# Expert weights loaded one by one at the ring's first turn, the scatter as two fp32r products, and a last quarter in halves

## The chip, the cores and the metric

One core of one Trainium2 chip runs the program. The metric is the device time of one execution in microseconds (us), as the median of several runs. The profile is of one execution. TensorE (PE in the rows; PEld is its weight load), VectorE (DVE), ScalarE (ACT), GpSimd (POOL) and SyncE (SP) each work through an own list of instructions and meet through semaphores.

## The reference

One decoder layer on x of 256 tokens by 1024, all float32: a mixer stage (sparse attention, pooling, short convolution, merged by gates and projected), then a mixture of experts, then a final RMSNorm. The change touches the mixture of experts and the first steps of the final norm:

```python
# 4 groups of 8 experts; each token takes one group and the best 2 experts in it
combine = jnp.einsum('nk,nke->ne', top_w, jax.nn.one_hot(expert_id, N_EXPERTS))
for e in range(N_EXPERTS):                       # 32
    h = jax.nn.silu(xt @ w1[e]) * (xt @ w3[e])   # 1024 -> 256
    out = out + combine[:, e:e + 1] * (h @ w2[e])  # 256 -> 1024
```

## The kernel before, in words

**Stages.** The mixer stage fills about the first 207 us. Routing follows to 220.5 us, then the experts. The experts' weights (three matrices of 1 MB for each of 32 experts) are read once, 96 chunks of 1 MB (128 partitions by 2048 float32).

**The ring.** `ring` has 22 slots of one chunk (`SLOTS`, line 42). The first 22 chunks are loaded one by one during the mixer stage as its slots come free (`early`, L508 to L511). All later ones go out in pairs, two chunks in one transfer, in SyncE's loops (L577 to L579, and L588 to L590 for the second half of the experts): the pair (c, c+1) waits until TensorE has counted up `expert_used` for the chunk that sat in the slot of c+1 before (`earlier(c + 1) + 1`). Only the last two chunks of a round go singly (L580 to L582, L592 to L595).

**Blocks.** The experts are worked in 8 blocks of 4 experts (`EB`), each expert with room for 32 tokens (`CAP`), so that a block has 128 rows. Four blocks are a round (`ROUND`), `j` is the block within it, and a round has 48 chunks, 12 for each block: q = 0 to 7 are the rows of w1 and w3 for one eighth of the model's width each, q = 8 to 11 the columns of w2 in four quarters of 256. In each block TensorE (L1736 to L1803) does, in this order:

- transposes of the combine weights of the block's rows (L1742, into bank 1, copied to `cmbT` by VectorE in L1312);
- q = 0 to 7: eight matmuls of 32 columns each group against the chunk (L1758). Before q = 1 and q = 2 it gathers the tokens of the second half of the width (`gather`, L1719, products with the 0/1 matrix `sel`), which VectorE copies (L1309). In the last block of a round two idle matmuls (`keep_busy`, L1368) stand after each of q = 4, 5 and 6;
- gathers 0 and 1 for the next block, after `sel_step`; the transposes of the hidden rows (L1774), for which ScalarE has done the silu (L894) and VectorE the product (L1317); gather 2; ScalarE copies the transposed rows (L896);
- second(0), gather 3, second(1), combine(0), second(2), combine(1), second(3), combine(2), combine(3). `second` (L1785) multiplies a quarter of w2 into bank 4 or 5, ScalarE copies it to `yN` (L901). `combine` (L1795) multiplies the combine weights `cmbT` with `yN` in plain float32 for each token tile t, into bank 6 + t; VectorE adds the result to `h` (L1323). A combine waits for the adds of the combine before it, since there are two banks.

**The end.** When the last quarters are added, ScalarE squares `h` in pieces (L920), GpSimd and VectorE multiply with the final gain (L675, L1349), VectorE sums the mean squares (L1351, L1354), GpSimd takes the power of -0.5 (L677), ScalarE and VectorE scale (L938, L1358), and four transfers write the output (L599, L940).

A matmul in plain float32 shows as two instructions in the trace, one in fp32r as one.

Of the kernel before, what the change touches and what calls it, by code (L numbers as in the profile page):

```python
# [5 lines left out]
ALU = mybir.AluOpType  # L6
# [28 lines left out]
NQT = D // QC  # L35
CAP = 32
# [5 lines left out]
SLOTS = 22  # L42
GATES = HEADS * 3
# [80 lines left out]
def build(nc, x, params, consts, front, projs, small, wgrp, vecs, routerw, routerb, experts, out):  # L124
    with ExitStack() as ctx:
# [103 lines left out]
        yN = gab[:].rearrange("p a c -> p (a c)")  # L229
# [13 lines left out]
        cmbT = vflat[:, 0:256]  # L243
# [31 lines left out]
        expert_in = [sem(f"expert_in{i}") for i in range(SLOTS // 2)]  # L275
        last_in = sem("last_in")
        expert_used = sem("expert_used")
# [98 lines left out]
        yn_done = sem("yn_done")  # L376
        gained = sem("gained")
# [86 lines left out]
        def second_out(qt, rows):  # L464

            return bank[4 + qt % 2][rows, 0:QC]

        def combined(t):

            return bank[6 + t][:, 0:QC]  # L470
# [4 lines left out]
        def _(sp):  # L475
# [104 lines left out]
            for c, sem_in in ((NC - 2, expert_in[AT[NC - 2] // 2]), (NC - 1, last_in)):  # L580
                sp.wait_ge(expert_used, earlier(c) + 1)
                sp.dma_start(ring[:, AT[c]], single(c)).then_inc(sem_in, 16)  # L582
# [4 lines left out]
            with sp.Fori(1, passes * (NB // ROUND)) as r:  # L587
# [4 lines left out]
                for c, sem_in in ((NC - 2, expert_in[AT[NC - 2] // 2]), (NC - 1, last_in)):  # L592
                    sp.wait_ge(expert_used, r * NC + (earlier(c) + 1))
                    sp.dma_start(ring[:, AT[c]], rounds[bass.ds(r % (NB // ROUND), 1), c // NQ, c % NQ // 2, :, c % 2 * ECHUNK:(c % 2 + 1) * ECHUNK]
                                 .rearrange("o p c -> (o p) c")).then_inc(sem_in, 16)  # L595
# [7 lines left out]
        def _(pool):  # L603
# [69 lines left out]
            for qt, c in ((1, slice(0, 2 * QC)), (2, slice(2 * QC, 3 * QC))):  # L673
                pool.wait_ge(add_done, passes * (NT * NQT * NB) + (NT * qt + 1 - NT))
                nc.gpsimd.tensor_tensor(fin[:, 1, c], h[:, 1, c], fing[:, c], ALU.mult).then_inc(gained_most, 1)  # L675
            pool.wait_ge(means_done, 2)
# [3 lines left out]
        def _(act):  # L680
# [226 lines left out]
            with act.Fori(0, passes * NB - 1) as b:  # L907
                hidden(b + 1)
                for qt in range(NQT):
                    second_copy(b + 1, qt)  # L910
# [4 lines left out]
            def last_square(n, t):  # L915

                qt, c0, c1, scratch = ((1, 0, 2 * QC, (kv[:, 512:1024], qflat[:, 0:512])), (2, 2 * QC, 3 * QC, (sl1, hN)),
                                       (3, 3 * QC, D, (flat(selw), flat(hT))))[n]
                act.wait_ge(add_done, passes * (NT * NQT * NB) + (NT * qt + t - NT))
                nc.scalar.activation(scratch[t], h[:, t, c0:c1], ACT.Square,  # L920
# [9 lines left out]
            for n in (1, 2):  # L930
# [4 lines left out]
            act.wait_ge(gained_most, 2)  # L935
# [7 lines left out]
        def _(dve):  # L943
            for s1 in (hn_done,):
                dve.sem_inc(s1, 1)
            dve.sem_inc(add_done, 5)
# [359 lines left out]
            def gathered(b):  # L1306
# [5 lines left out]
                nc.vector.tensor_copy(cmbT, bank[1][:, 0:T]).then_inc(cmb_done, 1)  # L1312

            def through(b):
# [4 lines left out]
                for qt in range(NQT):  # L1319
                    for t in range(NT):  # L1320
                        dve.wait_ge(comb_done, b * (NT * NQT) + (NT * qt + t + 1))
                        hv = h[:, t, qt * QC:(qt + 1) * QC]
                        nc.vector.tensor_tensor(hv, hv, combined(t), ALU.add).then_inc(add_done, 1)  # L1323
# [601 lines left out]
```

## Time and profile before

| | us |
|---|---|
| median of 3 runs | 423.47 |
| the runs | 423.47, 424.98, 423.26 |
| the profiled execution | 424.43 |
| its span | 422.6 |
| TensorE busy (share of the span) | 392.2 (93%) |
| VectorE busy | 200.6 (47%) |
| ScalarE busy | 141.8 (34%) |
| transfers, mean over the span | 332 GB/s |
| first expert matmul | 220.91 |
| last add to h ends | 415.68 |

The profiled execution took 424.43 us, 1.83 us more than its span, the time from the first to the last recorded instruction. All stretches below are counted from the start of the span. The page cuts the span into 40 slices of 10.6 us; the GB/s line gives what the transfers moved in each.

### The profile page before, as it was taken

To read this page: it belongs to the slowest core of one execution; us is meant where nothing else is said; L and a number is where in the kernel's file an instruction comes from. 1 tells how busy PE (TensorE), PEld (TensorE's weight loads), DVE (VectorE), ACT (ScalarE), POOL (GpSimd) and SP (SyncE) were. 2 spreads that over 40 slices of the span, in tenths; PEclk is the share of its full clock that TensorE was granted. 3 is DMA by queue.
4 is the path that set the end of the run, shared out by engine and by line. 5 is a ranking of instruction groups with operands and counts; after the bars stand their busy time and mean duration, and the time that the engine had idled before them with its cause. 6 is when DMAs were issued, how large, how long until landed. Compare 5 with 4: busy or idle time off the path is not lost.

```text
span 422.6 us, 7127 instructions
## 1 busy us (share of the span) xinstructions
PE 392.2 (93%) x2826; PEld 263.9 (62%) x2826; DVE 200.6 (47%) x392; ACT 141.8 (34%) x257; POOL 20.1 (5%) x39
## 2 busy tenths in 40 slices
PE   6999999999999999999989999999999779679792
PEld 5998988677777777878765545453546335135251
DVE  3847574999888595673362323231222203112113
ACT  6734352638555535341430303030303012011014
POOL 3010000200000000000510000000000000000002
PEclk9999999999999999999999999999999989899898
DMA  8999999534352485569987999999999999999962
GB/s 295 421 406 352 399 382 395 198 136 158 106 186 99 152 347 200 205 243 365 420 359 268 433 425 426 410 424 426 426 428 428 426 426 430 426 428 426 430 267 99
DMA packets 16440, 140.29 MB, mean 332 GB/s; under 512 B 2081, under 2 KB 2465, under 8 KB 5025
## 3 DMA queue, kind: packets, MB, share of 16 engines
q1 hardware_dynamic: 15264, 138.07, 81.1%
q10 hardware_dynamic: 1152, 1.88, 1.2%
q8 instruction: 17, 0.28, 0.3%
q14 instruction: 7, 0.05, 0.0%
HBM read 138.90 MB, written 1.05 MB: 331 GB/s over the span
## 4 chain that ended last, share of the span: by engine, by line
PE 73%; DMA 18%; DVE 6%; issue 1%; POOL 0%; ACT 0%; POOLq 0%; DVEq 0%; SPq 0%
DMA ring<-in_experts 17%; PE bank L1758 10%; PE bank L1719 5%; PE bank L1785 5%; PE bank L1795 5%; PE bank L1525 5%; PE bank L1526 4%; PE bank L1527 4%; PE bank L1383 4%; PE bank L1384 4%; PE bank L1385 4%; PE bank L1646 2%; PE bank L1368 2%; PE bank L1647 2%; PE bank L1648 2%; PE bank L1487 1%
## 5 line engine op out<-in xcount | busy, mean ns | idle before, releaser
L1758 PE MATMUL bank<-ring,kv 128*32 128x512 f32 x512 | 65.9, 630 | 12.9 <-DMA ring<-in_experts 12.8
L458 DVE TENSOR_TENSOR part<-ring,part 128x2048 fp32r<-128x2048 f32 (+1 forms) x26 | 57.4, 2213 | 18.7 <-ACT part L451 18.6
L451 ACT CAST part<-ring 128x2048 fp32r<-128x2048 f32 (+1 forms) x26 | 48.0, 1847 | 32.5 <-DMA ring<-in_front 32.5
L1323 DVE TENSOR_TENSOR h<-h,bank 128x256 f32<-128x256 f32 x64 | 26.9, 421 | 60.6 <-PE bank L1795 60.3
L1719 PEld LDWEIGHTS bank<-qcur,att 128*128 128x128 f32 x256 | 31.6, 191 | 24.2 <-issue 24.2
L1758 PEld LDWEIGHTS bank<-ring,kv 128*32 128x32 f32 x512 | 13.7, 112 | 42.1 <-issue 29.7
L1525 PE MATMUL bank<-part,xhi 128*128 128x512 f32 x96 | 39.2, 408 | 0.0
L894 ACT ACTIVATE cw<-bank 128x256 f32<-128x256 f32 x8 | 3.1, 384 | 105.4 <-PE bank L1758 105.4
L1719 PE MATMUL bank<-qcur,att 128*128 128x128 f32 x256 | 38.4, 288 | 0.0
L1527 PE MATMUL bank<-part,xlo 128*128 128x512 f32 x96 | 37.5, 391 | 0.0
L1526 PE MATMUL bank<-part,xhi 128*128 128x512 f32 x96 | 37.5, 391 | 0.0
L1383 PE MATMUL bank<-xhi,part 128*128 128x256 f32 x128 | 36.6, 286 | 0.5 <-DVE xlo L971 0.5
L1785 PE MATMUL bank<-ring,hidT 128*32 128x256 f32 x512 | 34.3, 385 | 2.9 <-DMA ring<-in_experts 2.8
L1795 PE MATMUL bank<-gab,vbd 128*128 128x256 f32 x128 | 36.2, 405 | 0.7
L1384 PE MATMUL bank<-xlo,part 128*128 128x256 f32 x128 | 36.2, 283 | 0.0
L1385 PE MATMUL bank<-xhi,part 128*128 128x256 f32 x128 | 36.2, 283 | 0.0
L1795 PEld LDWEIGHTS bank<-gab,vbd 128*128 128x128 f32 x128 | 21.0, 188 | 16.1 <-DVE h L1323 9.6
L1317 DVE TENSOR_TENSOR vbd<-cw,bank 128x256 f32<-128x256 f32 x8 | 3.4, 420 | 56.2 <-ACT cw L894 56.2
L901 ACT COPY gab<-bank 128x256 f32<-128x256 f32 x32 | 11.9, 372 | 47.9 <-PE bank L1785 47.9
L1383 PEld LDWEIGHTS bank<-xhi,part 128*128 128x128 f32 x128 | 24.5, 192 | 1.7 <-DVE xlo L971 0.9
L1385 PEld LDWEIGHTS bank<-xhi,part 128*128 128x128 f32 x128 | 24.5, 192 | 0.0
L1384 PEld LDWEIGHTS bank<-xlo,part 128*128 128x128 f32 x128 | 24.5, 192 | 0.0
(250 smaller groups left out, 549.9 us busy)
## 6 DMA issues: line engine op xcount, KB each, us to landing
ring<-in_experts SPq DMA_DIRECT2D x35, 2048.0 KB, 27.6
ring<-in_front SPq DMA_DIRECT2D x28, 1024.0 KB, 5.6
ring<-in_experts SPq DMA_DIRECT2D x26, 1024.0 KB, 8.7
ring<-in_front SPq DMA_DIRECT2D x4, 512.0 KB, 6.9
ring<-in_projs SPq DMA_DIRECT2D x4, 512.0 KB, 5.0
ring<-in_front SPq DMA_DIRECT2D x2, 560.0 KB, 8.7
h<-in_x SPq DMA_DIRECT2D x2, 512.0 KB, 3.8
con<-in_vecs ACTq DMA_DIRECT2D x2, 512.0 KB, 7.5
```

The source lines that it names most:

```text
L451: nc.scalar.copy(high(n, half)[:, 0:c].bitcast(F32R), raw(n, half)[:, 0:c]).then_inc(hi_done, 1)
L458: nc.vector.tensor_tensor(low(n, half)[:, 0:c].bitcast(F32R), raw(n, half)[:, 0:c], high(n, half)[:, 0:c], ALU.subtract).then_inc(split_do ...
L1383: mm(dst, whi, ahi, start=start, stop=False)
L1384: mm(dst, whi, alo, start=False, stop=False)
L1385: return mm(dst, wlo, ahi, start=False, stop=stop)
L1525: mm(bank[t][:], XH[:, kk, cols], whi[:, k], start=(kk == 0), stop=False)
L1526: mm(bank[t][:], XH[:, kk, cols], wlo[:, k], start=False, stop=False)
L1527: ins = mm(bank[t][:], XL[:, kk, cols], whi[:, k], start=False, stop=(kk == KT - 1))
L1719: ins = mm(bank[2 + k // 4][:, (k % 4) * P:(k % 4 + 1) * P], xn2[:, t, k * P:(k + 1) * P], flat(sel[:, t]), start=(t == 0), stop=(t == NT ...
L1758: ins = mm(bank[0][CAP * e:CAP * (e + 1)], xgT[:, q, CAP * e:CAP * (e + 1)], expert(j, q, e), start=(q == 0), stop=(q == NQ1 - 1))
L1785: ins = mm(second_out(qt, slice(CAP * e, CAP * (e + 1))), hT[:, ht, CAP * e:CAP * (e + 1)], second_weights(j, qt, ht, e), start=(ht == 0), ...
L1795: mm(combined(t), cmbT[:, t * P:(t + 1) * P], yN[:, qt * QC:(qt + 1) * QC], start=True, stop=True).then_inc(comb_done, 1)
```

## The change

- **Single loads.** The first six transfers at the ring's second turn (chunks 22 to 27 of the first round) go out singly, each after its own slot's `expert_used`. The pairs start at chunk 28.
- **Last quarter in halves.** The w2 columns are worked in five pieces: three quarters of 256 and two halves of 128. The last chunk of a round comes in two transfers of 0.5 MB, each with its own semaphore, in a layout in which each half is contiguous.
- **Moved transposes.** The combine weights' transposes go from the block's start to behind q = 2.
- **Moved gathers.** In the last block of a round the four gathers for the next block stand behind q = 4, 5, 6 and 7, and `keep_busy` is gone there. In the other blocks they stay.
- **Scatter in fp32r.** VectorE makes `cmbT` a 0/1 matrix (rounded exactly in fp32r) and puts each row's combine weight into a column `share` (two instructions where there was one). ScalarE's copy scales by `share` and rounds to fp32r; VectorE computes what the rounding left (`low_part`, new); `combine` adds two fp32r products, of the rounded and of the rest.
- **Order at the end.** VectorE does low_part(p) before the adds of p - 1. In the last block of a round TensorE does second 0, 1, combine 0, 1, second 2, combine 2, second 3, second 4, combine 3, combine 4. The final squares, gains and mean sums have one more piece each.

```diff
+PIECES = ((0, 256), (256, 512), (512, 768), (768, 896), (896, 1024))
+NP = len(PIECES)
+SINGLES = 6
...
-        cmbT = vflat[:, 0:256]
+        cmbT = over("cmbT", [P, T], "vbd")[:]
+        share = stat[:, 40:41]
...
@@ SyncE
-            for c in range(SLOTS, NC - 2, 2):
+            for c in range(SLOTS, SLOTS + SINGLES):
+                sp.wait_ge(expert_used, earlier(c) + 1)
+                sp.dma_start(ring[:, AT[c]], single(c)).then_inc(expert_in[AT[c] // 2] if c % 2 else single_in, 16)
+            for c in range(SLOTS + SINGLES, NC - 2, 2):
                 sp.wait_ge(expert_used, earlier(c + 1) + 1)
                 sp.dma_start(slots_of(c), experts[c // NQ, c % NQ // 2]).then_inc(expert_in[AT[c] // 2], 16)
...
+            def last_chunk(r):
+
+                for i, sem_in in ((0, last_half_in), (1, last_in)):
+                    sp.dma_start(ring[:, AT[NC - 1], i * (SLOT // 2):(i + 1) * (SLOT // 2)],
+                                 halves[bass.ds(r, 1), i].rearrange("o p c -> (o p) c")).then_inc(sem_in, 16)
@@ ScalarE
-            def second_copy(after, qt):
-
-                act.wait_ge(ye_full, after * NQT + (qt + 1))
-                nc.scalar.copy(yN[:, qt * QC:(qt + 1) * QC], second_out(qt, slice(0, P))).then_inc(yn_done, 1)
+            def second_copy(after, p):
+
+                act.wait_ge(ye_full, after * NP + (p + 1))
+                act.wait_ge(cmb_done, after)
+                nc.scalar.activation(yN[:, columns(p)].bitcast(F32R), second_out(p, slice(0, P)), ACT.Copy, scale=share).then_inc(yn_done, 1)
@@ VectorE
-                nc.vector.tensor_copy(cmbT, bank[1][:, 0:T]).then_inc(cmb_done, 1)
+                nc.vector.tensor_scalar(cmbT.bitcast(F32R), bank[1][:, 0:T], 0.0, None, ALU.is_gt)
+                nc.vector.tensor_reduce(share, bank[1][:, 0:T], AX.X, ALU.add).then_inc(cmb_done, 1)
...
+                def low_part(p):
+
+                    dve.wait_ge(yn_done, b * NP + (p + 1) + 1)
+                    nc.vector.scalar_tensor_tensor(low_out(p).bitcast(F32R), second_out(p, slice(0, P)), share, yN[:, columns(p)],
+                                                   ALU.mult, ALU.subtract).then_inc(ylo_done, 1)
...
+                low_part(0)
+                for p in range(1, NP):
+                    low_part(p)
+                    add(p - 1)
+                add(NP - 1)
@@ TensorE
-                    pe.wait_ge(sel_done, b + 1)
-                    pe.wait_ge(hT_done, b + 1)
-                    for t in range(NT):
-                        ins = nc.tensor.transpose(bank[1][:, t * P:(t + 1) * P], flat(selw[:, t]), ident)
-                    ins.then_inc(cmb_full, 1)
...
-                        if j == ROUND - 1 and 4 <= q < NQ1 - 1:
-                            pe.wait_ge(add_done, b * (NT * NQT) + 5)
-                            keep_busy(2, ident, con[:, K_TRI:K_TRI + 2 * P])
-
-                    pe.wait_ge(sel_step, b + 2)
-                    gather(0, 1)
+                        if q == 2:
+                            pe.wait_ge(sel_done, b + 1)
+                            pe.wait_ge(hT_done, b + 1)
+                            for t in range(NT):
+                                ins = nc.tensor.transpose(bank[1][:, t * P:(t + 1) * P], flat(selw[:, t]), ident)
+                            ins.then_inc(cmb_full, 1)
+                        if j == ROUND - 1 and q >= 4:
+                            pe.wait_ge(sel_step, b + 2)
+                            gather(q - 4)
+
+                    if j < ROUND - 1:
+                        pe.wait_ge(sel_step, b + 2)
+                        gather(0, 1)
...
-                        pe.wait_ge(yn_done, b * NQT + (qt + 1) + 1)
-                        pe.sem_inc(expert_used, 1)
+                        pe.wait_ge(ylo_done, b * NP + (p + 1))
+                        if p != NP - 2:
+                            pe.sem_inc(expert_used, 1)
                         for t in range(NT):
-                            pe.wait_ge(add_done, b * (NT * NQT) + (NT * qt + t + 4))
-                            mm(combined(t), cmbT[:, t * P:(t + 1) * P], yN[:, qt * QC:(qt + 1) * QC],
-                               start=True, stop=True).then_inc(comb_done, 1)
+                            pe.wait_ge(add_done, b * (NT * NP) + (NT * p + t + 6))
+                            picked = cmbT[:, t * P:(t + 1) * P].bitcast(F32R)
+                            mm(combined(p, t), picked, yN[:, columns(p)].bitcast(F32R), start=True, stop=False)
+                            mm(combined(p, t), picked, low_out(p).bitcast(F32R), start=False, stop=True).then_inc(comb_done, 1)
 
                     second(0)
-                    gather(3)
-                    for qt in range(1, NQT):
-                        second(qt)
-                        combine(qt - 1)
-                    combine(NQT - 1)
+                    if j < ROUND - 1:
+                        gather(3)
+                    second(1)
+                    combine(0)
+                    if j == ROUND - 1:
+                        combine(1)
+                    second(2)
+                    combine(2 if j == ROUND - 1 else 1)
+                    second(3)
+                    if j < ROUND - 1:
+                        combine(2)
+                    second(4)
+                    combine(3)
+                    combine(4)
```

## Rows read from the trace of the kernel before

**Rows 1.** The page: GB/s in 40 slices; one kind of transfer, size, us to landing

```profile
GB/s 295 421 406 352 399 382 395 198 136 158 106 186 99 152 347 200 205 243 365 420 359 268 433 425 426 410 424 426 426 428 428 426 426 430 426 428 426 430 267 99
...
ring<-in_front SPq DMA_DIRECT2D x28, 1024.0 KB, 5.6
```
**Rows 2.** The chain that ended last, in order of time: start, us, what

```profile
363.18 32.15 DMA ring<-in_experts
...
396.57 2.01 PE bank L1368 x4
```
**Rows 3.** Stretches: length, busy PE, PEld, DVE, ACT, POOL, clock, DMA share, GB/s

```profile
221.00:222.00 1.00, 1.00 (x9) 0.16 (x9) 0.00 (x0) 0.00 (x0) 0.00 (x0) 1.00 0.00 0
397.00:398.00 1.00, 1.00 (x4) 0.68 (x3) 0.00 (x0) 0.00 (x0) 0.00 (x0) 0.50 1.04 442
409.00:410.00 1.00, 1.00 (x8) 0.59 (x11) 0.49 (x2) 0.27 (x1) 0.00 (x0) 1.00 0.08 33
```
**Rows 4.** Timeline, 217 to 225 and 242 us: start, us, engine, line, operation, count, idle before

```profile
217.48 2.02 PE L1728 MATMUL bank<-qcur,att 128*128 128x128 f32 x16 [0.16 <-DVE qcur L1290]
...
219.56 1.28 ACT L894 ACT_TABLE_LOAD   x1 [0.55 <-issue]
...
220.54 0.44 PE L1742 MATMUL bank<-con,otmp 128*128 128x128 f32 x2 [1.04 <-DVE otmp L1298]
...
220.91 1.07 PE L1758 MATMUL bank<-ring,kv 128*32 128x512 f32 x8
...
221.91 1.16 PE L1719 MATMUL bank<-qcur,att 128*128 128x128 f32 x8
...
223.00 1.06 PE L1758 MATMUL bank<-ring,kv 128*32 128x512 f32 x8
...
224.12 0.33 SPq L579 DMA_DIRECT2D ring<-in_experts  x1
...
241.61 1.06 PE L1758 MATMUL bank<-ring,kv 128*32 128x512 f32 x8
```
**Rows 5.** Timeline, 362 to 371 and 404 to 423 us, same columns

```profile
366.04 3.30 PE L1758 MATMUL bank<-ring,kv 128*32 128x512 f32 x16 [3.06 <-DMA ring<-in_experts]
...
404.26 0.38 ACT L894 ACTIVATE cw<-bank 128x256 f32<-128x256 f32 x1 [19.53 <-PE bank L1758]
...
406.12 1.07 PE L1785 MATMUL bank<-ring,hidT 128*32 128x256 f32 x16
...
407.25 0.37 ACT L901 COPY gab<-bank 128x256 f32<-128x256 f32 x1 [1.19 <-PE bank L1785]
...
408.76 1.13 PE L1795 MATMUL bank<-gab,vbd 128*128 128x256 f32 x4
...
409.50 0.85 DVE L1323 TENSOR_TENSOR h<-h,bank 128x256 f32<-128x256 f32 x2 [4.40 <-PE bank L1795]
...
414.10 0.73 PEld L1795 LDWEIGHTS bank<-gab,vbd 128*128 128x128 f32 x4 [0.48 <-DVE h L1323]
...
414.83 0.85 DVE L1323 TENSOR_TENSOR h<-h,bank 128x256 f32<-128x256 f32 x2 [0.36 <-PE bank L1795]
...
416.32 0.16 DVE L1354 TENSOR_TENSOR stat<-stat 128x2 f32<-128x2 f32 x1
416.56 0.71 POOL L677 TENSOR_TENSOR stat<-stat 128x2 f32<-128x2 f32 x1 [1.28 <-DVE stat L1354]
```
**Rows 6.** Groups by line and shape: busy us, mean ns, idle before

```profile
L971 DVE SCALAR_TENSOR_TENSOR xlo<-bank,prm,xhi 128x256 fp32r<-128x256 f32 x8 | 3.5, 477 | 0.1
...
L706 ACT ACTIVATE xhi<-bank,prm 128x256 fp32r<-128x256 f32 x8 | 3.3, 492 | 0.1
...
L1193 DVE TENSOR_TENSOR pcw<-otmp,con 128x128 f32<-128x128 f32 x2 | 0.5, 288 | 0.0
```
**Rows 7.** Timeline of TensorE at 52 us: two fp32r matmuls in a row

```profile
51.89 0.28 PE L1384 MATMUL bank<-xlo,part 128*128 128x256 f32 x1
52.01 0.28 PE L1385 MATMUL bank<-xhi,part 128*128 128x256 f32 x1
```

More of the change, by code:

```diff
@@ L462, in xT, with columns, low_out, second_out @@
             return bank[(0, 1, 2, 3, 6, 7, 5, 5)[k]][:, (k == 7) * T:((k == 7) + 1) * T]
[L464 to L470, printed above, removed]
+        def columns(p):
+            return slice(*PIECES[p])
+        def low_out(p):
+            c0, c1 = PIECES[p]
+            return ylo[c0 // 512][:, c0 % 512:c0 % 512 + c1 - c0]
+        def second_out(p, rows):
+            return bank[4 + p % 2][rows, 0:PIECES[p][1] - PIECES[p][0]]
+        def combined(p, t):
+            return bank[6 + t][:, 0:PIECES[p][1] - PIECES[p][0]]
         block = ctx.enter_context(nc.Block())
@@ L591, in _ @@
                                  .rearrange("o p c -> (o p) c")).then_inc(expert_in[AT[c] // 2], 16)
[L592 to L595, printed above, removed]
+                sp.wait_ge(expert_used, r * NC + (earlier(NC - 2) + 1))
+                next_to_last(r % (NB // ROUND))
+                sp.wait_ge(expert_used, r * NC + (earlier(NC - 1) + 1))
+                last_chunk(r % (NB // ROUND))
             for half, t in ((0, 0), (0, 1), (1, 0)):
@@ L672, in _ @@
             pool.wait_ge(vec_in, 32)
-            for qt, c in ((1, slice(0, 2 * QC)), (2, slice(2 * QC, 3 * QC))):
-                pool.wait_ge(add_done, passes * (NT * NQT * NB) + (NT * qt + 1 - NT))
+            for p, c in ((1, slice(0, 512)), (2, columns(2)), (3, columns(3))):
+                pool.wait_ge(add_done, passes * (NT * NP * NB) + (NT * p + 1 - NT))
                 nc.gpsimd.tensor_tensor(fin[:, 1, c], h[:, 1, c], fing[:, c], ALU.mult).then_inc(gained_most, 1)
-            pool.wait_ge(means_done, 2)
+            pool.wait_ge(means_done, 3)
             nc.gpsimd.tensor_tensor(stat[:, 30:32], stat[:, 28:30], stat[:, 32:34], ALU.pow).then_inc(rstd_last, 1)
@@ L908, in _ @@
                 hidden(b + 1)
-                for qt in range(NQT):
-                    second_copy(b + 1, qt)
+                for p in range(NP):
+                    second_copy(b + 1, p)
                 gathered_copy(b + 1)
@@ L929, in _ @@
             second_copy(blocks, 3)
-            for n in (1, 2):
+            second_copy(blocks, 4)
+            for n in (1, 2, 3):
                 for t in range(NT):
@@ L1775, in _, with second @@
                     ins.then_inc(hT_full, 1)
-                    gather(2)
+                    if j < ROUND - 1:
+                        gather(2)
                     pe.wait_ge(hT_done, b + 2)
-                    def second(qt):
-                        have_expert(j, NQ1 + qt)
+                    def second(p):
+                        if j == ROUND - 1 and p == NP - 2:
+                            pe.wait_ge(last_half_in, bb * 16 + 16)
+                        else:
+                            have_expert(j, NQ1 + PIECES[p][0] // QC)
@@ L1899 @@
         w2.transpose(0, 4, 3, 2, 1, 5).reshape(NB, NQ2, P, ECHUNK)], axis=1)
+    halves = experts[:, NQ - 1].reshape(NB, P, HT * EB, 2, QC // 2).transpose(0, 1, 3, 2, 4).copy()
+    experts[:, NQ - 1] = halves.reshape(NB, P, ECHUNK)
+    ends = np.stack([experts[:, NQ - 2], halves.transpose(0, 2, 1, 3, 4).reshape(NB, P, ECHUNK)], axis=1).reshape(NB, P, 2 * ECHUNK)
     experts = experts.reshape(NB, NQ // 2, 2, P, ECHUNK).transpose(0, 1, 3, 2, 4).reshape(NB, NQ // 2, P, 2 * ECHUNK)
+    experts[ROUND - 1::ROUND, NQ // 2 - 1] = ends[ROUND - 1::ROUND]
     arrays = {
```

67 lines of the change are left out of this document (42 added, 25 removed).

## The prediction

> **What bounds the kernel now.** I read the slices first: from the 23rd on, the transfers move 424 to 434 GB/s (two slices 410 and 426) until the last two [rows 1]. In the slices before, at 211 to 232 us, there is a hole of 359 and 268. So the experts are bound by reading 96 MB, and what counts is where this stream starts, and what follows its last bytes. The stretches show both ends: nothing moves at 221 to 222 us, and the stream is almost over at 409 to 410 [rows 3]. The timeline says why: the first transfer of the ring's second turn is issued at 224.12, right after chunk 1 is used up at 224.06; chunk 0 had been used at 221.98 [rows 4]. The chain of waits shows the other end: TensorE stands before transfers from 363.18 to 395.33, and from there to the last add it is TensorE's own work that sets the time [rows 2, 5]. A pair of chunks lands every 4.89 us (waits that end at 366.04 and at 395.38 are six pairs apart [rows 2, 5]), so 2.45 us a chunk. By that step the last pair of w1 and w3 lands at 400.27, the first pair of w2 at 405.16, chunk 10 at 407.61 and chunk 11 at 410.05. Yet second(0) starts only at 406.12 and the last add ends at 414.83 + 0.85 = 415.68 [rows 5]: TensorE is late there, by gathers, idle matmuls and plain float32 products.
>
> **Start of the stream.** Two things come earlier. The single load needs chunk 0 alone: 224.06 - 221.98 = 2.08 us. And the transposes that stood ahead of chunk 0 waited for VectorE's weights until 220.54 [rows 4]; now TensorE can begin chunk 0 once it has left the first gathers (217.48 + 2.02 = 219.50) and entered its loop. No row shows that entry alone on TensorE. Bounds: 0, so 219.5, and the old wait's end, 220.5. ScalarE needs 0.55 us between its copy and the loop's first instruction [rows 4]; I take 0.5, so chunk 0 starts at 220.0 in place of 220.91. Sum 2.08 + 0.9 = 3.0 us, with 2.5 and 3.5 as ends. The following singles keep the stream fed: chunk 1 is free 2.1 us after chunk 0 (1.0 matmuls and 1.09 gathers [rows 4]), against 2.45 us that a chunk takes, chunk 2 two more after that, later ones about 1 us apart. TensorE's 20.7 us for an early block (220.91 to 241.61 [rows 4]) against 12 x 2.45 = 29.4 of the stream leaves the later pairs free early too. The six singles themselves cost nothing as long as others are queued: that is the slice of 420 GB/s, where singles run as well [rows 1].
>
> **Extra work in the other blocks: 0.** VectorE gets a reduction and five low parts more a block (some 2.6 us), and four fp32r products in place of four plain halves of products save TensorE about half of 1.06 us per combine [rows 5, 7]. It all lies beside the stream, as every block has 29.4 us. By the ladder worked out below, a block's last combine is issued some 5.5 us after its last pair lands, and 4.2 us more go to the next block's q = 0 and 1 with their gathers: 9.7, just within the 9.8 us to the landing of q = 2. Were it a few us more, the 2.9 us that TensorE waits for q = 4 would still hide it. The transposes behind q = 2 make VectorE wait there for them, and behind that wait stand the 0/1 matrix, the sum (0.42 each, as every 256-wide op), and the selection for the next block, for which the last block's gathers now wait: it is ready about 2.5 us after q = 2 lands, and the first gather comes over 5 us after it. On SyncE's queue five transfers more are issued (0.33 us each [rows 4]), all well ahead of their data's turn.
>
> **The last block.** All landings come 3.0 us earlier: q = 4 at 392.4, q = 6 at 397.3, second(0)'s chunk at 402.2, the last half at 407.1. Idle matmuls go (they took 2.01 us at half clock once [rows 2]), and gathers of 0.55 us take their place between chunks. From 397.3: 1.0 + 0.5 + 1.0 us for q = 6, a gather and q = 7, 0.13 to the silu, and as now 1.86 from there to second(0) (404.26 to 406.12 [rows 5]): ready at 401.8. So second(0) starts at 402.2, by its transfer, 3.9 us earlier than now.
>
> Then a longer ladder. second takes 1.0 us, the copy starts 0.13 behind it [rows 5]. The copy is now scaled from a column: 0.37 as a plain copy [rows 5], 0.49 in the row of the same form [rows 6]; I take 0.48. low_part is the form of L971, 0.48 [rows 6]; pieces of 128 take 0.38 and 0.33 (VectorE has 0.29 for an op of 128 [rows 6]). Adds 0.42 and 0.29. An fp32r product follows the last by 0.12 and ends 0.28 after its start [rows 7], so an add can start 0.47 behind its combine, where it now is 0.74 [rows 5]. VectorE's end reaches TensorE in 0.06 (an add ends at 414.05, the weight load is at 414.10). No row has an fp32r product of 128 columns; between 0.06 and 0.27 apart, I take 0.10, as its weights' load overlaps as in rows 7. Working it through:
> - second 0 and 1 to 404.20; copy 1 to 404.82; low 1 to 405.35; adds of 0 to 406.11; combine 1 must wait for their banks, to 406.41.
> - second 2 to 407.41. Its chunk landed at 404.6, so the transfer is not the wait. Copy 408.03, low 2 408.56, adds of 1 to 409.32, combine 2 to 409.62.
> - second 3 to 410.21, second 4 to 410.80; both halves are there since 407.1. Copy 3 410.73, low 3 411.11, adds of 2 411.87, low 4 412.20, adds of 3 412.70, combine 4's first product done 412.90, its adds 413.48.
>
> Last add 413.5 in place of 415.7. From the start of second(0) it is 11.3 us now against 9.6 before: the new order gives back 1.7 of 3.9. Behind the last add one more mean step (0.26, the distance of such steps, L1354 at 416.32) less 0.1 for smaller squares: the power starts at 414.5 where it was 416.56 [rows 5], the rest is equal. Span 422.6 - 2.0 = 420.6, time 424.43 - 2.0 = 422.4.
>
> **Against the median.** The profiled run was 0.96 above the median of 423.47. In it the clock was at 0.50 at 397 to 398 [rows 3], which made q = 6 start at 401.1 in place of its landing at 400.3: 0.8 us that the new order does not pay, since it has slack there. I put that to the profiled run alone and the other 0.16 to both: 422.2 us, which is 0.3% under the median. Changes within 0.5% (2.1 us) are about what the measurement can't tell from none.
>
> **A rule to weigh.** Singles ran at the stream's rate where several were queued [rows 1]. The Trainium skill (DMA: Bandwidth & Descriptors, Rules for kernel authors and Anatomy of one DMA) asks for transfers of at least 1 MiB and gives each about 2 us of fixed cost. By that page five more transfers (three for the singles, one half in each round), if none overlapped, would be 10 us more; it adds that issuing early hides the cost, and it speaks against the halves above all.
>
> **Rivals.**
> 1. The ladder is shorter, up to the halves' purpose, that the last bytes set the end. For it: VectorE and ScalarE may overlap more, and low ends of 0.42 and 0.37 for low part and copy take 0.6 off, an entry at 219.5 up to 0.4 more: 421.2. If only the last half at 407.1 counted: 0.6 + 0.5 + 0.4 + 0.4 + 0.6 to the last add at 409.6, and 418.3. Against: second(2) is 1.8 us behind its landing by the ladder. Chance 0.28, 418.3 to 421.3.
> 2. The change gives only the single load's 2.08, since TensorE's loop entry takes the whole microsecond that the moved transposes should free: 0.9 more, 423.1. Chance 0.10.
> 3. Half clock once in the tail. After 3.06 us of idleness 16 matmuls took 3.30 us [rows 5], where 2.0 do at full clock [rows 4]. The gaps between combines (up to 1.6 us) are shorter, but TensorE is only half busy. One such dip costs about 1.6 (3.3 us at half rate): 423.8. Chance 0.08.
> 4. The other side: the clock stays at its lower level (1.2 GHz) from second(0) to the end, as no idle matmuls hold it. TensorE's part of the ladder is 3.6 us of seconds and about 1.8 of combines; doubled, 5.4 more: 427.6. It decides from 3.4 us of TensorE's ladder at that level, over half of it. Chance 0.04.
> 5. Each of the five extra transfers pays alone, at most 5.6 - 2.45 = 3.15 us by a chunk loaded with little else in the queue [rows 1]: 422.2 + 15.8 = 438.0. Chance 0.02.
> The forecast has 0.48.
>
> **Numbers.** Faster by over 0.5% (under 421.35): rival 1 and the lower edge of the forecast, 0.33. Slower (over 425.6): rivals 4 and 5 and a little of 3, 0.08. Within: 0.59. The range 420.0 to 424.3 leaves out the best third of rival 1 and the worst of 3 to 5.
>
> **What would show it.** First load of the second turn at about 221.1 instead of 224.1; the stream's end 3 us earlier; second(0) of the last block near 402.2; second(2) over 1.5 us behind its chunk; the last add near 413.5. It is wrong if TensorE waits for the last half (then the ladder was overpriced), if the copy or low part is far from 0.48, or if the clock in the last 12 us is not 1.0.

## The result, and the profile after

| | before | after |
|---|---|---|
| median (18 runs each) | 424.35 | 425.25 |
| lowest and highest | 423.26, 426.21 | 424.85, 425.96 |
| the profiled execution | 424.43 | 425.27 |
| its span | 422.6 | 422.8 |

The ratio is 1.0023, with a 95% interval of 1.0015 to 1.0032: a loss of 0.9 us that is clear of the spread and smaller than the 0.5% within which the prediction counts a change as none. It is 3 us above the forecast and outside the range. (With 18 runs the kernel before has a median 0.9 above that of the three runs shown first.) Times below are us.

The timeline of after at the start of the experts, and at chunk 27's use in block 2 (start, length, engine, line, operation, count, idle before):

```profile
219.59 1.06 PE L1810 MATMUL bank<-ring,kv 128*32 128x512 f32 x8
...
220.71 2.42 SPq L598 DMA_DIRECT2D ring<-in_experts  x2
...
266.51 0.44 PE L1820 MATMUL bank<-con,otmp 128*128 128x128 f32 x2
...
266.88 4.50 PE L1810 MATMUL bank<-ring,kv 128*32 128x512 f32 x40
...
268.01 2.57 SPq L601 DMA_DIRECT2D ring<-in_experts  x3
```

The first load of the second turn goes out at 220.71, 3.4 earlier than in [rows 4]. But the pair (40, 41) goes out at 268.01, just after TensorE has worked chunk 27 (q = 3 of block 2, from 266.88). The stretches show what lies between (columns as in [rows 3]: length, five engines, clock, DMA share, GB/s); first four long ones, then single microseconds:

```profile
219.00:226.00 7.00, 6.96 (x55) 3.26 (x58) 2.31 (x6) 1.35 (x2) 0.00 (x0) 1.00 0.84 304
226.00:263.00 37.00, 35.55 (x367) 19.31 (x360) 13.88 (x39) 9.33 (x18) 0.00 (x0) 1.00 1.00 417
263.00:272.00 9.00, 9.00 (x77) 3.68 (x76) 2.34 (x6) 0.38 (x1) 0.00 (x0) 1.00 0.88 335
272.00:390.00 118.00, 99.69 (x951) 52.35 (x953) 36.33 (x101) 21.67 (x43) 0.00 (x0) 0.97 1.01 427
...
267.00:268.00 1.00, 1.00 (x12) 0.30 (x13) 1.00 (x3) 0.00 (x0) 0.00 (x0) 1.00 0.61 246
268.00:269.00 1.00, 1.00 (x12) 0.26 (x8) 0.50 (x2) 0.00 (x0) 0.00 (x0) 1.00 0.39 115
269.00:270.00 1.00, 1.00 (x16) 0.35 (x12) 0.00 (x0) 0.00 (x0) 0.00 (x0) 1.00 1.07 213
```

The same four stretches of before:

```profile
219.00:226.00 7.00, 5.96 (x51) 3.08 (x53) 1.66 (x4) 1.30 (x2) 0.00 (x0) 1.00 0.41 119
226.00:263.00 37.00, 36.81 (x332) 18.52 (x324) 10.32 (x25) 8.04 (x16) 0.00 (x0) 1.00 0.99 422
263.00:272.00 9.00, 9.00 (x78) 3.78 (x75) 1.78 (x4) 0.09 (x1) 0.00 (x0) 1.00 1.00 406
272.00:390.00 118.00, 104.88 (x862) 52.22 (x862) 26.05 (x61) 18.71 (x39) 0.00 (x0) 0.97 1.01 427
```

Length times GB/s, added up, says how far each stream is. At 226 after is 7 x (304 - 119) = 1295 ahead, at 427 GB/s 3.0 us. At 272 it is 1295 - 37 x 5 - 9 x 71 = 471 ahead, 1.1 us. Behind that both run at 427. A second hole, at 267 to 271, has taken most of the lead.

The end, in after's timeline:

```profile
394.64 1.60 PE L1810 MATMUL bank<-ring,kv 128*32 128x512 f32 x8 [2.38 <-DMA ring<-in_experts]
...
404.55 1.93 PE L1848 MATMUL bank<-ring,hidT 128*32 128x256 f32 x32 [0.84 <-DMA ring<-in_experts]
405.68 0.47 ACT L939 ACTIVATE yN<-bank,stat 128x256 fp32r<-128x256 f32 x1 [1.56 <-PE bank L1848]
406.18 0.48 DVE L1363 SCALAR_TENSOR_TENSOR ylo<-bank,stat,yN 128x256 fp32r<-128x256 f32 x1 [3.04 <-ACT yN L939]
...
408.72 1.07 PE L1848 MATMUL bank<-ring,hidT 128*32 128x256 f32 x16
...
412.00 1.08 PE L1848 MATMUL bank<-ring,hidT 128*32 128x128 f32 x32
...
415.14 0.62 DVE L1371 TENSOR_TENSOR h<-h,bank 128x128 f32<-128x128 f32 x2 [0.20 <-PE bank L1861]
...
416.77 0.71 POOL L714 TENSOR_TENSOR stat<-stat 128x2 f32<-128x2 f32 x1 [1.29 <-DVE stat L1409]
```

Chunk q = 4 is waited for until 394.64, only 0.7 earlier than 395.38. second(0) starts at 404.55 by its transfer, the last add ends at 415.76: a ladder of 11.2. The last add is where it was (415.68 [rows 5]).

### The profile page after: what moved, and what is told of

The parts are those of the page before. It is cut to its first block, busy times and chain, and to the rows that moved or that the text cites. A ratio compares the mean times of both kernels' runs of the same rounds, so it can differ in the third digit from the quotient of the medians.

```text
span 422.8 us, 7620 instructions
## 1 busy us (share of the span) xinstructions
PE 383.0 (91%) x2962; PEld 263.3 (62%) x2962; DVE 217.8 (52%) x457; ACT 147.4 (35%) x269; POOL 20.0 (5%) x40
## 4 chain that ended last, share of the span: by engine, by line
PE 66%; DMA 21%; DVE 7%; issue 2%; ACT 2%; DVEq 0%; POOL 0%; SPq 0%; POOLq 0%; PEldq 0%
DMA ring<-in_experts 20%; PE bank L1810 9%; PE bank L1580 5%; PE bank L1778 5%; PE bank L1581 4%; PE bank L1582 4%; PE bank L1848 4%; PE bank L1438 4%; PE bank L1439 4%; PE bank L1440 4%; PE bank L1860 2%; PE bank L1701 2%; PE bank L1703 2%; PE bank L1702 2%; PE bank L1542 1%
## 5 line engine op out<-in xcount | busy, mean ns | idle before, releaser
L1778 PEld LDWEIGHTS bank<-qcur,att 128*128 128x128 f32 x256 | 33.0, 197 | 30.1 <-issue 29.2
L1363 DVE SCALAR_TENSOR_TENSOR ylo<-bank,stat,yN 128x256 fp32r<-128x256 f32 (+1 forms) x40 | 17.2, 431 | 46.5 <-ACT yN L939 46.5
L1778 PE MATMUL bank<-qcur,att 128*128 128x128 f32 x256 | 40.5, 296 | 0.0
L1848 PE MATMUL bank<-ring,hidT 128*32 128x256 f32 (+1 forms) x640 | 35.2, 342 | 3.5 <-DMA ring<-in_experts 3.0
L1860 PE MATMUL bank<-yN,cmbT 128*128 128x256 f32 (+1 forms) x80 | 25.1, 335 | 10.3 <-DVE h L1371 9.2
L1810 PEld LDWEIGHTS bank<-ring,kv 128*32 128x32 f32 x512 | 12.6, 110 | 34.5 <-issue 20.7
L939 ACT ACTIVATE yN<-bank,stat 128x256 fp32r<-128x256 f32 (+1 forms) x40 | 17.2, 431 | 47.6 <-PE bank L1848 47.5
L1860 PEld LDWEIGHTS bank<-yN,cmbT 128*128 128x128 f32 x80 | 15.0, 187 | 22.4 <-DVE h L1371 16.8
L1371 DVE TENSOR_TENSOR h<-h,bank 128x256 f32<-128x256 f32 (+1 forms) x80 | 26.1, 362 | 2.8 <-PE bank L1861 2.6
L1438 PEld LDWEIGHTS bank<-xhi,part 128*128 128x128 f32 x128 | 24.5, 192 | 1.7 <-DVE xlo L1011 0.9
L1848 PEld LDWEIGHTS bank<-ring,hidT 128*32 128x32 f32 x640 | 16.5, 109 | 13.3 <-ACT hidT L933 3.0
## 6 DMA issues: line engine op xcount, KB each, us to landing
ring<-in_experts SPq DMA_DIRECT2D x4, 512.0 KB, 29.4
```

The source lines that it names most:

```text
L1438: mm(dst, whi, ahi, start=start, stop=False)
L1778: ins = mm(bank[2 + k // 4][:, (k % 4) * P:(k % 4 + 1) * P], xn2[:, t, k * P:(k + 1) * P], flat(sel[:, t]), start=(t == 0), stop=(t == NT ...
L1810: ins = mm(bank[0][CAP * e:CAP * (e + 1)], xgT[:, q, CAP * e:CAP * (e + 1)], expert(j, q, e), start=(q == 0), stop=(q == NQ1 - 1))
L1848: ins = mm(second_out(p, slice(CAP * e, CAP * (e + 1))), hT[:, ht, CAP * e:CAP * (e + 1)], second_weights(j, p, ht, e), start=(ht == 0), s ...
L1860: mm(combined(p, t), picked, yN[:, columns(p)].bitcast(F32R), start=True, stop=False)
```

## Experiments

Each kernel was timed in five rounds. The ratios are to the kernel before as timed beside it: its median was 424.21 beside e1 to e4, 424.31 beside e5 and e7 to e9, and 424.44 beside e6 and e10 to e12. "Landing" is the start of q = 4 in the last block, "ladder" the time from second(0)'s start to the end of the last add, "outside" the median of time less span over its runs. Landing and ladder are from the profiled execution. Before and e2 are alike up to the last block and land 0.35 apart, so a few tenths in a landing say little by themselves.

| kernel | median | ratio, 95% interval | landing | second(0) | ladder | outside |
|---|---|---|---|---|---|---|
| before | 424.35 | 1 | 395.38 | 406.12 | 9.56 | 1.8 |
| after | 425.25 | 1.0023, 1.0015 to 1.0032 | 394.64 | 404.55 | 11.21 | 2.4 |
| e1_start | 424.4 | 0.9994, 0.9977 to 1.0011 | 395.16 | 407.22 | 9.57 | 1.8 |
| e2_gathers | 423.1 | 0.9969, 0.9954 to 0.9984 | 395.73 | 405.64 | 8.78 | 1.8 |
| e3_both | 422.5 | 0.9947, 0.9928 to 0.9965 | 395.06 | 404.96 | 8.79 | 1.8 |
| e4_both40 | 422.28 | 0.9941, 0.9919 to 0.9962 | 394.02 | 404.76 | 8.78 | 1.8 |
| e5_pairs | 425.38 | 1.0026, 1.0011 to 1.0040 | 394.77 | 404.67 | 11.2 | 2.45 |
| e6_after40 | 425.13 | 1.0014, 1.0002 to 1.0026 | 394.21 | 404.11 | 11.2 | 2.4 |
| e7_order | 423.98 | 0.9999, 0.9986 to 1.0011 | 394.92 | 404.85 | 9.81 | 2.45 |
| e8_halves | 424.35 | 0.9999, 0.9985 to 1.0013 | 395.95 | 405.86 | 9.11 | 2.2 |
| e9_fp32r | 421.6 | 0.9937, 0.9916 to 0.9958 | 393.90 | 404.69 | 9.46 | 1.8 |
| e10_pace40 | 421.36 | 0.9923, 0.9905 to 0.9941 | 393.07 | 402.99 | 9.4 | 1.8 |
| e11_busy | 420.9 | 0.9912, 0.9894 to 0.9929 | 392.86 | 402.77 | 9.44 | 1.8 |
| e12_split | 422.49 | 0.9953, 0.9935 to 0.9970 | 394.36 | 404.26 | 9.44 | 1.9 |

One reading holds in all fourteen profiles: q = 4 of the last block lands 126.6 to 127.7 us after chunk 40 is issued (268.47 in before, 268.01 in after, 266.84 in e9, 265.28 in e11), whenever the stream started.

### The parts one by one

**e1_start**: the kernel before with the six singles and the moved transposes.

```diff
-            for c in range(SLOTS, NC - 2, 2):
+            for c in range(SLOTS, NC - 2):
+                if c in SINGLE:
+                    sp.wait_ge(expert_used, earlier(c) + 1)
+                    sp.dma_start(ring[:, AT[c]], single(c)).then_inc(expert_in[AT[c] // 2] if c % 2 else single_in, 16)
```

> The kernel before with the six single loads and the transposes moved behind q = 2, nothing else. My theory (a second gate): the first load of the second turn goes out 3.4 us earlier, as in the changed kernel, but chunk 40 has to wait for chunks 26 and 27 to be used up, whose use comes only about 1 us earlier, so a hole opens in the stream near 267 to 270 us and the pair q = 4, 5 of the last block lands only 0.7 to 1.3 us earlier than the 395.4 of before. Time 0.7 to 1.3 us under the kernel before. Rival (the stream simply runs earlier and it is the tail that lost all): no hole, the pair lands 3.4 us earlier, and the time falls by 3.4 us, as TensorE works through from there to the end.

It gained nothing, where 0.7 to 1.3 us had been expected. Its stream is 7 x (276 - 119) ahead at 226, 2.6 us, and falls to 311 GB/s in 263 to 272 (before 406). Chunk 40 goes out no earlier than before, at 268.59, though TensorE started chunk 0 0.97 earlier (219.94):

```profile
219.94 1.06 PE L1761 MATMUL bank<-ring,kv 128*32 128x512 f32 x8 [0.20 <-issue]
...
240.93 1.07 PE L1761 MATMUL bank<-ring,kv 128*32 128x512 f32 x8
...
267.09 0.44 PE L1771 MATMUL bank<-con,otmp 128*128 128x128 f32 x2
...
268.59 2.53 SPq L585 DMA_DIRECT2D ring<-in_experts  x3
```

A block takes 20.99 here against 20.70 in before (220.91 to 241.61 [rows 4]), and in block 2 the transposes, behind q = 2, now stand ahead of chunk 27. Two longer blocks and one pair of transposes, 2 x 0.29 + 0.37 = 0.95, are the 0.97 again. So the moved transposes take back at chunk 27 what they give at chunk 0. In the profiled execution, the longest of its twelve (425.53, 1.1 above their median), TensorE was late besides, with q = 4 and q = 5 at 1.94 each, at half clock:

```profile
395.16 1.94 PE L1761 MATMUL bank<-ring,kv 128*32 128x512 f32 x8 [2.37 <-DMA ring<-in_experts]
399.03 1.94 PE L1761 MATMUL bank<-ring,kv 128*32 128x512 f32 x8
```

**e2_gathers**: before with the four gathers behind q = 4 to 7 of a round's last block, and no idle matmuls there.

```diff
-                            keep_busy(2, ident, con[:, K_TRI:K_TRI + 2 * P])
...
+                            pe.wait_ge(sel_step, b + 2)
+                            gather(q - 4)
```

> The kernel before with the four gathers of a round's last block behind q = 4 to 7 and without the idle matmuls there, nothing else. Theory (TensorE is late at the end of the kernel before, and the plain float32 combine is the short way): second(0) of the last block starts when its chunk lands, near 405.2, and the last add follows 8.9 us later (the 9.6 of before less the gather between second 0 and 1), near 414.1 where it was 415.7. Time 1.2 us (0.8 to 1.6) under the kernel before. Rival (the idle matmuls held the clock up): the granted clock falls below 1.0 behind 400 us and the time is the same or longer.

A gain of 1.25 against the kernel before, by two things that its timeline shows: second(0) now waits for its transfer (0.85 of idleness, start 405.64 in place of 406.12), and the ladder is 0.8 shorter, as gather(3) no longer stands in it.

**e3_both**: both together.

> The two edits together, scatter and last quarter as before. Theory: the gains add, 1.2 + 1.0, so 2.2 us (1.5 to 2.9) under the kernel before, and some 3 us under the changed kernel, which differs from it only in the fp32r scatter, the halves and the order at the end. Rival (the fp32r scatter and the halves are not what costs): within 0.5 us of the changed kernel.

0.6 less than e2 (the intervals overlap): all that the start of the stream 3.3 us earlier is worth once TensorE isn't late. Its landing is 0.67 earlier than e2's.

**e4_both40**: e3 with chunks 40 to 43 loaded singly as well, so that chunk 40 waits for chunk 26 alone.

```diff
-SINGLE = tuple(range(22, 28))
+SINGLE = tuple(range(22, 28)) + (40, 41, 42, 43,)
```

> As the one before, and chunks 40 to 43 go out singly too, so that chunk 40 waits for chunk 26 alone. Theory of the second gate: chunk 40 is issued 1.2 us earlier, the hole near 267 us shrinks by that, and everything behind it moves: 1.2 us less than with the two edits alone. Rival (the dip near 267 us is the memory's or the queue's own): the same time as with the two edits alone, and the hole as long.

The landing came 1.04 earlier than in e3, as a gate at chunk 40 demands; the time only 0.2 (the intervals overlap). Here second(0) waits 0.46 for the copy of the hidden rows instead of a transfer: TensorE had worked q = 4 and 5 at half clock (1.93 and 1.94) and was late again.

**e5_pairs** and **e6_after40**: after without any singles, and after with the four more.

```diff
-SINGLES = 6
+SINGLES = 0
```

> The changed kernel with pairs at the ring's second turn instead of the six single loads; all else as changed. Theory of the second gate: the stream starts 2.1 us later, but it no longer runs dry (or only as briefly as before the change) when it comes to chunk 40, so the last block's chunks land within 0.4 us of where they do in the changed kernel, and the time is within 0.5 us of its 425.25. Rival (the single loads are worth their 2.1 us, whatever happens at chunk 40): 2 us slower, 427.3.

> The changed kernel with chunks 40 to 43 also loaded singly, so that chunk 40 waits for chunk 26 alone. Theory (the stream's second hole is the wait of chunk 40 for slot 4, so its place is set by TensorE's pace in blocks 0 to 2): chunk 40 goes out 1.2 us earlier and the chunks of the last block land about 1 us earlier; in the plain pair of kernels with this difference they did, 394.02 for 395.06. TensorE could be ready for second(0) at 404.2 where it now starts at 404.55, so the time falls by only 0.2 to 0.7 us unless the clock stays up. Rival (the hole is the memory's own): landings and time as in the changed kernel.

e5 is the sharpest test of the second gate. Its stream moves 186 GB/s in 219 to 226 against 304, so it is 1.9 us behind, and 379 against 335 in 263 to 272; at 390 it has moved 97 (us times GB/s) less, 0.2 us. Its landing and its time are after's within 0.13. The six singles bought a longer hole. In e6 the hole is shallower (381 GB/s) and the landing 0.4 earlier, the time 0.1 lower, which the runs can't tell from none. Its chunk 40 went out 1.3 earlier (266.69).

### The last block and the scatter

**e7_order**: after with the other blocks' order in the last block too.

```diff
                     second(1)
                     combine(0)
-                    if j == ROUND - 1:
-                        combine(1)
                     second(2)
-                    combine(2 if j == ROUND - 1 else 1)
+                    combine(1)
                     second(3)
-                    if j < ROUND - 1:
-                        combine(2)
+                    combine(2)
                     second(4)
```

> The changed kernel, with TensorE's order in the last block as in the others: second 0, 1, combine 0, second 2, combine 1, second 3, combine 2, second 4, combine 3, combine 4. Theory of the ladder: combine 1 no longer holds second 2 back while VectorE works, and the same working that gave 11.3 us from second(0) to the last add gives 9.6 us for this order; 1.6 us less, 423.6. Rival (the fp32r scatter's own chain of copy, low part and two adds sets the end, whatever TensorE does between): no change, within 0.3 us of 425.25.

The new order alone costs 1.3 (intervals apart). In after, combine 1 stands ahead of second 2, and combine 2 ahead of seconds 3 and 4; e7 has the seconds under the copies and adds instead:

```profile
404.85 1.93 PE L1848 MATMUL bank<-ring,hidT 128*32 128x256 f32 x32 [0.85 <-DMA ring<-in_experts]
...
407.90 1.07 PE L1848 MATMUL bank<-ring,hidT 128*32 128x256 f32 x16
...
409.57 0.64 PE L1848 MATMUL bank<-ring,hidT 128*32 128x128 f32 x16
...
411.18 0.64 PE L1848 MATMUL bank<-ring,hidT 128*32 128x128 f32 x16
...
414.05 0.61 DVE L1371 TENSOR_TENSOR h<-h,bank 128x128 f32<-128x128 f32 x2 [0.20 <-PE bank L1861]
```

**e8_halves**: e3 with five pieces and the last chunk in two loads, the scatter still in plain float32, the order as in e7. (The lines are against after.)

```diff
+                        pe.wait_ge(yn_done, b * NP + (p + 1) + 1)
...
+                            mm(combined(p, t), cmbT[:, t * P:(t + 1) * P], yN[:, columns(p)], start=True, stop=True).then_inc(comb_done, 1)
```

> The kernel with both start and gather edits (422.5 us), and the last quarter in halves, but with the scatter in plain float32 as before and the order of the other blocks. Theory: with the plain scatter the tail is TensorE's own 8.8 us, and halves shorten only what follows the last product: copy by 0.1, combine by 0.5 less what is already hidden, adds by 0.26; 0.3 to 0.8 us less, 421.7 to 422.2. Rival (what the changed kernel loses outside its span, 2.4 us against 1.8, comes with the halves and their steps): as long as without halves or longer, with the span shorter and the time outside it 2.4.

It fell 1.85 behind e3, where 421.7 to 422.2 had been expected. Of that 0.9 is a later landing, 0.3 the ladder, 0.4 time outside the span, and the rest is spread over the run-to-run differences. The late landing is the second gate again. The transposes of the combine weights mark each block; in e8 they are 21.44 apart:

```profile
224.87 0.44 PE L1801 MATMUL bank<-con,otmp 128*128 128x128 f32 x2
246.31 0.44 PE L1801 MATMUL bank<-con,otmp 128*128 128x128 f32 x2
```

and for one microsecond of the hole its stream stands still:

```profile
267.00:268.00 1.00, 1.00 (x10) 0.20 (x2) 0.55 (x1) 0.00 (x0) 0.00 (x0) 1.00 0.28 115
268.00:269.00 1.00, 1.00 (x11) 0.29 (x13) 0.76 (x2) 0.00 (x0) 0.00 (x0) 1.00 0.18 66
269.00:270.00 1.00, 1.00 (x16) 0.39 (x12) 0.43 (x1) 0.00 (x0) 0.00 (x0) 1.00 0.00 0
```

**e9_fp32r**: e3 with the fp32r scatter and nothing of the halves (four quarters, one last load).

```diff
+                            picked = cmbT[:, t * P:(t + 1) * P].bitcast(F32R)
+                            mm(combined(t), picked, yN[:, qt * QC:(qt + 1) * QC].bitcast(F32R), start=True, stop=False)
+                            mm(combined(t), picked, low_out(qt).bitcast(F32R), start=False, stop=True).then_inc(comb_done, 1)
```

> The kernel with both start and gather edits (422.5 us), and the scatter in fp32r, with four quarters, no halves, and the order of the other blocks. Theory of the ladder: copy 0.48, low part 0.48 and the adds behind it in VectorE's order make 9.2 us from second(0) to the last add, where the plain scatter has 8.8; 0.3 to 0.6 us slower, 422.8 to 423.1, if the time outside the span stays at 1.8, and 423.4 to 423.7 if that comes with the fp32r scatter. Rival (fp32r saves TensorE half a microsecond a combine, so it is faster once it isn't held up by the order): 421.5 or less.

A loss was expected, for the longer ladder. The ladder is 0.67 longer, but the median is 0.9 lower than e3's (the intervals overlap, so the sign is less sure than the mechanism). The blocks are faster, 20.21 against e3's 20.99:

```profile
224.92 0.44 PE L1794 MATMUL bank<-con,otmp 128*128 128x128 f32 x2
245.13 0.44 PE L1794 MATMUL bank<-con,otmp 128*128 128x128 f32 x2
```

so the second gate opens 1.5 earlier (chunk 40 is issued at 266.84, in e3 at 268.34) and the stretch of 263 to 272 has 388 GB/s against e3's 339. The profiled execution (422.9, the slowest of its six) also shows half clock over more than half of the last block's first part: the granted clock was 0.50 from 394 to 400, after 2.38 of idleness.

**e10_pace40** and **e11_busy**: e9 with singles 40 to 43; and that with idle matmuls behind q = 3 of a round's last block.

```diff
+                        if j == ROUND - 1 and q == 3:
+                            pe.wait_ge(add_done, b * (NT * NQT) + 5)
+                            keep_busy(3, ident, con[:, K_TRI:K_TRI + 2 * P])
```

> The kernel with both start and gather edits and the fp32r scatter in four quarters (421.6 us), and chunks 40 to 43 loaded singly. Theory: its pace of 20.2 us a block already makes the hole shorter; the single loads take up to 1 us more off the stream. The last block's q = 4 lands near 393.0 where it was 393.9. But in the profile of that kernel the clock was at its lower level from 393.9 to 400.8 and TensorE, not the stream, set second(0). So the time falls by 0 to 1 us, 420.6 to 421.6. Rival (TensorE's lateness by the clock takes all): 421.6.

> The one before, and three idle matmuls (1.6 us) behind q = 3 of each round's last block, in the wait for q = 4. Theory of the clock: it fell after TensorE had stood still for 2.4 us there; with the idle matmuls it stays at 1.0, TensorE waits for each chunk, and second(0) starts when its chunk lands, near 403.0; 0.5 to 1.5 us less than the one before, and a smaller spread of the runs (1.65 us in the kernel with the fp32r scatter in four quarters). Rival (the idle matmuls delay q = 4 or don't hold the clock): the same time or up to 0.5 us more.

e11 is the fastest kernel of the study, 420.9 against 424.44 for the kernel before in the same series, ratio 0.9912: better than before and after both. Its hole is gone:

```profile
263.00:272.00 9.00, 8.98 (x80) 4.25 (x80) 2.63 (x6) 0.76 (x2) 0.00 (x0) 1.00 1.00 419
```

and TensorE is in time for each chunk of the last block at full clock, which the idle matmuls (L1397) carry over the wait for q = 4:

```profile
390.42 1.56 PE L1397 MATMUL bank<-con 128*128 128x256 f32 x6
392.86 1.06 PE L1784 MATMUL bank<-ring,kv 128*32 128x512 f32 x8 [0.88 <-DMA ring<-in_experts]
...
397.87 1.07 PE L1784 MATMUL bank<-ring,kv 128*32 128x512 f32 x8 [1.66 <-DMA ring<-in_experts]
...
402.77 1.93 PE L1822 MATMUL bank<-ring,hidT 128*32 128x256 f32 x32 [0.75 <-DMA ring<-in_experts]
```

e10, without them, has q = 4 and 5 at 1.77 and 1.43 in place of 1.06, yet its second(0) too starts by its transfer (402.99, after 0.75 of idleness), so its profile doesn't show a gain that the idle matmuls could bring. The steps e9 to e10 (0.2) and e10 to e11 (0.5) are each within the intervals, and what the idle matmuls are worth is not shown; from e3 to e11 it is 1.6, and there the intervals hardly touch (0.9928 and 0.9929).

**e12_split**: e9 with the last chunk of a round in two loads of 0.5 MB and nothing else of the halves.

```diff
-            for c, sem_in in ((NC - 2, expert_in[AT[NC - 2] // 2]), (NC - 1, last_in)):
...
+            for i, sem_in in ((0, last_half_in), (1, last_in)):
...
+                sp.dma_start(ring[:, AT[NC - 1], cols], single(NC - 1)[:, cols]).then_inc(sem_in, 16)
```

> The kernel with both start and gather edits and the fp32r scatter in four quarters (421.6 us), and a round's last chunk loaded in two transfers of 0.5 MB, both awaited before the last quarter; no other part of the halves. It asks where the 0.4 to 0.6 us outside the span come from that all kernels with halves have (2.2 to 2.45 against 1.8). Theory (they come with the second transfer and its semaphore): outside 2.2 us, time 422.0. Rival (they come with the longer programs of the five pieces): outside 1.8 us, time 421.6.

The ladder is e9's (9.44), time outside the span 1.9. So two loads and a second semaphore are not what adds 0.6 outside the span in after. What is left is the five pieces, by e8 (2.2 with plain products) and after (2.4 with fp32r), or the layout in which each half is contiguous, which all kernels with five pieces have and e12, with strided halves, has not; no run parts the two. The median is 0.9 over e9's with intervals that overlap, and its q = 4 landed 0.46 later than e9's though chunk 40 went out 0.2 earlier (266.62), which leaves open whether the split costs some tenths; it gains nothing.

## Why the prediction was wrong

The forecast for the profiled execution was 422.4, it took 425.27. Its steps in turn:

- **Start of the stream: right.** 3.0 early was forecast, with 3.5 as end; it was 3.4, chunk 0 starting at 219.59 (forecast 220.0). But the 1.3 us that TensorE gained there by the moved transposes it did not keep, see the third point.
- **"Leaves the later pairs free early too": this is the step that failed.** It compared rates, 20.7 a block against 29.4. But the ring is 22 slots, and chunks 40 to 43 return to slots 4 to 7 (AT, L71 of before), which chunks 26 to 29 hold: they are only 14 chunks on. So the pair (40, 41) waits until TensorE has used chunk 27 in block 2, which is two blocks and a half behind the start, whatever the stream does. In before that is at 266.49 + 1.92 = 268.4 (rows below), and the stream, started at 224.12, had delivered its chunks 22 to 39 (18 x 2.45 = 44.1) at about 268.2, an estimate from the prediction's step: the two just met, and only a shallow hole showed (328 GB/s at 270 to 272). After's stream is still 1295 - 185 = 1110 ahead at 263, 2.6 us, so by the same estimate it has them by about 265.6, and then it stands. The gate itself moved from 268.47 to 268.01. What passes it is this half microsecond and the tenths that the old meeting left: the landing of q = 4 came 0.7 earlier, not 3.0. e5 moves the start of the stream alone (2.2 later), and the landing stays. e4 and e10 (the gate at chunk 26: landings 1.0 and 0.8 earlier) and e9 (faster blocks, 1.2 earlier than e3) move the gate alone, and the landing follows.

The timeline of before, TensorE at q = 2 and 3 of block 2, and the issue of the pair (40, 41):

```profile
266.49 1.92 PE L1758 MATMUL bank<-ring,kv 128*32 128x512 f32 x16
...
268.47 2.78 SPq L579 DMA_DIRECT2D ring<-in_experts  x3
```

- **"Extra work in the other blocks: 0": wrong for blocks 0 to 2.** The cover named, the stream's 29.4 a block, isn't there before the second gate. There TensorE waits for no transfer, and every tenth in its blocks counts two to two and a half times. A block takes 20.70 in before and 20.99 with the transposes moved (e1, e3); from there 20.21 with the fp32r scatter (e9), 21.44 with the halves (e8), and 20.87 with both (after): the five pieces, each a copy, low part, product and add more, eat most of what fp32r saves, and 0.71 of after's block is TensorE's wait for VectorE's adds before two combines. So after's blocks are 0.17 longer than before's, and its 1.3 us at chunk 0 have shrunk to 0.46 at the issue of chunk 40. The prediction counted the moved transposes as 0.9 us gained; at the gate that decides they gain nothing (e1).
- **Ladder: right.** second(0) to the last add was put at 11.3 and took 11.21. Copy 0.47, low part 0.48, halves 0.37 and 0.35, as priced. second(2) began at 408.72, behind combine 1, not its transfer. The ladders of the table add up: the gathers taken out -0.8, fp32r +0.7, halves +0.3, new order +1.4. The prediction saw that the order gives time back, but not that every part but the gathers lengthens the end.
- **Last block.** second(0) was by its transfer, as forecast, at 404.55 in place of 402.2. The idle matmuls' place and the gathers' price behind q = 4 to 7 played no part, as forecast: TensorE was ready for second(0) 0.84 before its chunk.
- **Time outside the span: a term missing.** It was taken as the same 1.83 and is 2.4 in after.

Together: 404.55 - 402.2 = 2.35, -0.1 for the ladder, 0 behind it, +0.6 outside the span: 2.9, of 2.87. Against before: second(0) -1.6, ladder +1.65, 0.1 to the power, 0.6 outside, 0.8 in all. So the change's three parts for the end and its part for the start nearly cancel, and what tips it is outside the span.

Of the rivals none came: the gain of rival 2 (the single load alone) would also have been lost at the second gate, and a rival "the stream stands at the next reuse" was missing. The clock was at 0.50 for about 3 us at q = 4 and 5 (0.72 over 394 to 400), ahead of second(0) and so at no cost here: rival 3's dip, in a place with slack. Rival 5, each extra transfer pays alone, is far from the 425.25 measured, and e5 against after bears that out: six singles in place of three pairs changed neither landing nor time. The Trainium skill (DMA: Bandwidth & Descriptors, Rules for kernel authors) asks for at least 1 MiB a transfer. The singles, of 1024 KB, keep to that, and the page's fixed cost (Anatomy of one DMA) doesn't show where others are queued. The halves, of 0.5 MB, don't keep to it; e12 is the only run that has them alone, and tenths could hide there.

What stays open: why the kernels with five pieces take 0.4 to 0.6 more outside the span. The traces cover the span alone, and no run took the five pieces away from the last norm or from the experts alone, or gave four quarters the contiguous layout. In after this is 0.6 of the 0.8 us lost against before in the profiled executions.

## What to carry to other kernels

When a ring's first gate is opened earlier, follow the stream to every later reuse of a slot and write both times beside each, the stream's arrival and the consumer's release; the gain ends at the first where the consumer is last, and the consumer's pace up to there, not its average slack, is what must be shortened. Work moved out of the way at the start is still there: behind q = 2 the transposes came ahead of the next gate. A last tile cut in halves shortens the end only if the bytes set it; here the end was a chain of three engines, and each piece more added a link to it. Once the last chunks arrive earlier, TensorE can be late by half clock (in e4 and e9 second(0) waited for the hidden rows and no longer for its transfer). Idle matmuls in the wait kept the clock up in e11; that they shorten the time is not shown.

## What the runs showed of the hardware

- Half the columns did not halve an fp32r product. In after four products of 128 columns of one combine start 0.16, 0.12 and 0.11 apart; of 256 columns it was 0.22, 0.12 and 0.11 (406.95, 407.17, 407.29, 407.40):

```profile
259.59 0.33 PE L1860 MATMUL bank<-yN,cmbT 128*128 128x128 f32 x1
...
259.75 0.27 PE L1861 MATMUL bank<-ylo,cmbT 128*128 128x128 f32 x1
...
259.87 0.28 PE L1860 MATMUL bank<-yN,cmbT 128*128 128x128 f32 x1
...
259.98 0.27 PE L1861 MATMUL bank<-ylo,cmbT 128*128 128x128 f32 x1
```

- A wait of TensorE of 2.3 to 2.9 us before q = 4 of the last block was followed by half clock (granted 0.50, 1.2 GHz) in the profiles of all thirteen kernels that have it, but from another matmul on: e3 did q = 4 in 1.06 and q = 5 in 1.94, e4 both in 1.93 and 1.94, and e9 stayed low until 400. e11, idle 0.88 at that place and 1.66 at q = 6, didn't fall.
- The time outside the span is not a constant of the chip: 1.8 in eight kernels, 1.9 in e12, and 2.2 to 2.45 in the five-piece ones.
